# Own semaphores per stage, expert weights in 2 MB loads of 16 KB pieces, and layer 1's memory keys and values made in the first stage

## The chip, the cores and the metric

The kernel runs on one core of a Trainium2 chip. The metric is the device time of one execution in microseconds; a median of several executions is given. The engines of a core named below are TensorE (PE, with PEld for its weight loads), VectorE (DVE), ScalarE (ACT), GpSimd (POOL) and SyncE (SP). Inputs and output are float32.

## The reference

Two blocks run one after the other on 256 tokens of width 1024. The first has two layers. Each layer mixes the tokens (layer 0: a gated projection with a spatial gate over chunks of 128 tokens; layer 1: dilated attention), adds attention over 256 memory rows, normalises, and then runs a mixture of 16 experts, of which every token takes two. The second block (retention, sparse attention, a recurrent mixer, two feed-forward parts, two layers) is not touched by the change.

```
for layer in range(DEPTH):
    mk = (mem @ w_mem_k[layer]).reshape(B, M, MEM_HEADS, HEAD_DIM)
    mv = (mem @ w_mem_v[layer]).reshape(B, M, MEM_HEADS, HEAD_DIM)
    ...
    att = jnp.concatenate([mix, mo], -1) @ w_out
    x = layer_norm(ALPHA * x + att, ln1_g[layer], ln1_b[layer])
    expert, gate = route(h, w_router, b_router)
    ffn = moe_ffn(h, expert, gate, w_gate[layer], w_up[layer], w_down[layer])   # silu(x wg) * (x wu), then wd
    x = layer_norm(ALPHA * x + ffn, ln2_g[layer], ln2_b[layer])
```

Each of the 16 experts of a layer has three matrices of 1024 x 1024, 12 MB; a layer's experts are 201 MB.

## The kernel before

Every engine runs its own program, stage by stage: A (layer 0's mixing), moe0, B (layer 1's mixing), moe1, and two (the second block). The order is written out by hand; each engine's function of a stage has its prefix (`pe_a`, `s_a`, `v_a`, `g_a`, `sp_a` and so on).

Weights go through a ring of 8 slots of 1 MB (8 KB per partition). SP's program orders the loads: `load` (L485) waits until enough slots have been used (`s_used`), then orders a DMA into the slot. In A, B and two a load is a block of 256 columns, so its contiguous pieces are 1 KB. GpSimd relays: `freed` (L517) waits until a product is complete and adds to `s_used`. Products go to four PSUM banks in turn ("pieces"); a semaphore per bank says that it is full, another that it is free.

Stages A to moe1 share one set of semaphores and counters; at each stage's end all engines pad their counters to a multiple of the ring (`end_of_stream`). Stage two has its own set, and a ring of 5 slots.

An expert stage first routes (`pe_moe` from L1100, `v_moe` from L1259) and then loops over 8 pairs of experts, as many passes as the fullest expert needs (one here: CAP is 64 tokens). A turn of the loop: transposes of the gate matrix, the gather of the pair's tokens (X as TensorE's weights, `pair_rows` taking every second column), gate and up products with the two experts side by side in the columns of the array, transposes of h, down products, and the combine into four accumulating banks. Expert weights are loaded by `one` (L1419, the DMA at L1425) as 256 rows of 1024 values, 1 MB: partition p takes rows 2p and 2p + 1, one piece of 8 KB. TensorE adds to `s_half` when 2 MB (both experts) have been used, and GpSimd relays it. SP orders the first 8 loads of a stage ahead of its loop.

In A, ScalarE's last work is a square root for the norm; then `s_moe(0)` orders 20 small parameter loads and two norm loads (L1786, L776) and copies half of x's transposes (L636). Memory keys and values of a layer are made at the start of its own mixing stage by `memory_kv`; the transposed memory `MEMT` stays in the arena until then. In A's spatial gate (L845) each head has two matmuls of 64 columns, one per chunk. The arena is 21760 values per partition; during an expert stage its end is unused.

Of the kernel before, what the change touches and what calls it, by code (L numbers as in the profile page):

```python
# [29 lines left out]
I32 = mybir.dt.int32  # L30
# [4 lines left out]
P = 128  # L35
# [5 lines left out]
HD = 64  # L41
# [26 lines left out]
RAW, HIGHS = 5, 3  # L68
BANKS = 4
# [11 lines left out]
for _k, _v in PV_ROWS.items():  # L81
# [8 lines left out]
        ("pe", "jobs"): 24, ("pe", "pieces"): 12, ("pe", "v2p"): 1,  # L90
        ("v", "jobs"): 24, ("v", "pieces"): 12,
        ("s", "jobs"): 24, ("s", "pieces"): 12,
        ("g", "jobs"): 24, ("g", "pieces"): 12, ("g", "half"): 9,
        ("sp", "jobs"): 24,
    },
    "moe1": {
        ("pe", "jobs"): 24, ("pe", "pieces"): 12, ("pe", "v2p"): 1,
        ("v", "jobs"): 24, ("v", "pieces"): 12,
        ("s", "jobs"): 24, ("s", "pieces"): 12,
        ("g", "jobs"): 24, ("g", "pieces"): 12, ("g", "half"): 9,  # L100
        ("sp", "jobs"): 24,
# [97 lines left out]
def build(nc, a, out, regions=("A", "moe0", "B", "moe1", "two"), layers_two=LAYERS):  # L199
    (c1_at, _), (c2_at, _) = constants()  # L200
    NC = max(max(v[1] for v in c1_at.values()), max(v[1] for v in c2_at.values()))
    with ExitStack() as ctx:
# [57 lines left out]
        def stage_semaphores(tag):  # L260
# [3 lines left out]
                    [sem(f"slot_loaded{s}{tag}") for s in range(SLOTS)],  # L264
# [4 lines left out]
        FIRST, SECOND = stage_semaphores(""), stage_semaphores("_two")  # L269
        s_full, s_free, s_slot, s_acc_full, s_acc_free, s_used, s_v2p, s_a2p, s_v2a, s_a2v = FIRST  # L270
# [11 lines left out]
        s_half = sem("expert_rows_used")  # L282
        s_load = {n: sem(f"loaded_{n}") for n in
# [6 lines left out]
        class Engine:  # L290
# [13 lines left out]
            def second(self):  # L304

                use(SECOND)
                self.jobs, self.pieces = Ring(RAW), Ring(BANKS)
                self.next_high, self.in_high = 0, {}
                for k, v in self.c.items():
                    if not k.startswith("l_"):  # L310
                        v.n, v.base = 0, 0
# [52 lines left out]
            def jobs_pad_check(self):  # L364
                assert self.pieces.n % BANKS == 0 and self.jobs.n % SLOTS == 0, (self.name, self.pieces.n, self.jobs.n)
# [40 lines left out]
        class Tensor(Engine):  # L406
# [8 lines left out]
            def hold(self, b=0):  # L415


                self.mm(ps[:, b, 0:1], ident, ident[:, 0:1], start=True, stop=True)

# [19 lines left out]
            def gemm_tok(self, act, kc=KC, n=BLK, col=0, width=None, slot=None):  # L439
# [9 lines left out]
                for t in range(T):  # L449
                    for k in range(kc):  # L450
                        last = self.mm(ps[:, b, t * BLK:t * BLK + n], act[:, k, t * P:(t + 1) * P],
                                       w[:, k, col:col + n], start=(k == 0), stop=(k == kc - 1))
                last.then_inc(s_full[b], 1)
# [17 lines left out]
        class Stream(Engine):  # L471
            before = None

            def second(self):

                self.before = self.jobs
                super().second()

            def first_slots_free(self):

                n = self.jobs.n
                if self.before is not None and n <= RAW:
                    self.e.wait_ge(FIRST[5], self.before.rounds * SLOTS + self.before.n + n)

            def load(self, src, n, width):  # L485
# [3 lines left out]
                self.first_slots_free()  # L489
                self.e.wait_ge(s_used, self.in_use())  # L490
# [3 lines left out]
            def in_use(self):  # L494
# [3 lines left out]
                return n if isinstance(r, int) and r == 0 else r * SLOTS + n  # L498
# [76 lines left out]
        QM, MK, MV = lay(2, SEQ), lay(2, SEQ), lay(T, MEM_W)  # L575
# [8 lines left out]
        lay = Layout(after_mem)  # L584
        XG, PM, PG, PGT = lay(KC, P), lay(T, P), lay(T, P), lay(SEQ)
# [16 lines left out]
        NPASS = sb("n_passes", [1, 1], I32)  # L602
# [37 lines left out]
        def pe_scores(heads, q, k):  # L640
            for h in heads:
                b = pe.take()
                pe.e.wait_ge(s_free[b], pe.emptied())
                for t in range(T):
                    last = pe.mm(ps[:, b, t * SEQ:(t + 1) * SEQ], q(h)[:, t * P:(t + 1) * P], k(h),
                                 start=True, stop=True)
                last.then_inc(s_full[b], 1)
# [135 lines left out]
        def memory_kv(l):  # L783
# [2144 lines left out]
```

## Time and profile before

| | us |
|---|---|
| median of 3 executions | 3056.08 (3055.98 to 3057.8) |
| the profiled execution | 3066.24 |
| its span, first to last instruction | 3064.4 |
| TensorE busy | 2724.0 (89%) |
| VectorE busy | 1158.8 (38%) |
| ScalarE busy | 786.6 (26%) |

The page divides the span into 40 slices of 76.6 us. The granted clock of TensorE was 0.954 of full speed over the span. By the timeline, stage A ends near 161 us, the first expert loop runs from 196 to 665 us, B ends near 835 us, the second loop runs from 868 to 1338 us, and the second block fills the rest. Idle time of an engine that is not the bound costs nothing; what counts is which wait ends last.

### The profile page before, as it was taken

The page shows a single profiled execution, that of the slowest core. Times are in us where ns is not written, and L with a number is a line of the kernel's source. Part 1 is how long each engine was busy: PE and PEld are TensorE (multiplying, and loading weights), DVE is VectorE, ACT ScalarE, POOL GpSimd, SP SyncE. Part 2 cuts the span into 40 slices and gives each one's busy share as a digit, 9 for nine tenths or more (in the row PEclk, how much of TensorE's full clock was granted, in tenths as well). Part 3 has the DMA queues.
Part 4 walks back from the last instruction along what each step waited for, and adds up shares of the span by engine and source line. Part 5 has one row for each costly group of instructions (what it writes and reads, how often), then busy time and mean ns, then how long its engine had stood idle before and what let it go on. Part 6 is the DMA issues. An engine that isn't in the chain of part 4 may idle for free.

```text
span 3064.4 us, 44961 instructions
## 1 busy us (share of the span) xinstructions
PE 2724.0 (89%) x18948; PEld 2089.2 (68%) x18948; DVE 1158.8 (38%) x1768; ACT 786.6 (26%) x971; POOL 0.2 (0%) x4
## 2 busy tenths in 40 slices
PE   7878888889678888869989899989899898999898
PEld 6643433348434333339989789889799897898897
DVE  0220100123311001035556756445445567564454
ACT  1110101102201011024334442243343343422433
POOL 0000000000000000000000000000000000000000
PEclk9879999999889999989999899999899998998999
DMA  7159999993269999975554332346455543322453
GB/s 246 71 223 420 421 422 422 422 395 110 83 250 419 422 422 422 421 274 193 174 168 141 110 111 71 111 140 204 144 190 169 164 152 110 111 71 84 154 176 124
DMA packets 286112, 684.46 MB, mean 223 GB/s; under 512 B 11898, under 2 KB 217474, under 8 KB 236548
## 3 DMA queue, kind: packets, MB, share of 16 engines
q1 hardware_dynamic: 279776, 669.03, 58.3%
q10 hardware_dynamic: 6180, 13.14, 1.2%
q8 instruction: 123, 2.02, 0.3%
q14 instruction: 33, 0.27, 0.0%
HBM read 681.08 MB, written 1.05 MB: 223 GB/s over the span
## 4 chain that ended last, share of the span: by engine, by line
PE 72%; DMA 15%; DVE 7%; ACT 2%; issue 1%; DVEq 1%; ACTq 1%; SPq 0%; POOLq 0%; PEldq 0%
PE psum L421 70%; DMA weight_ring<-in_w_down 8%; DMA weight_ring<-in_w_up 7%; PE psum L429 2%; DVEq L543 1%; DVE weight_ring_parts L1563 1%; DVE arena_parts L1633 1%; DVE small L666 1%; DVE arena L664 1%; ACT h_tok L1535 0%; SPq L1425 0%; DVE arena L1356 0%; ACT L770 0%; DVE arena L2600 0%; ACTq L865 0%
## 5 line engine op out<-in xcount | busy, mean ns | idle before, releaser
L421 PE MATMUL psum<-weight_ring,arena 128*64 128x512 f32 (+1 forms) x3584 | 798.8, 564 | 126.1 <-DMA weight_ring<-in_w_down 43.3
L421 PEld LDWEIGHTS psum<-weight_ring,arena 128*64 128x64 f32 (+1 forms) x3584 | 346.7, 144 | 552.8 <-issue 537.9
L421 PE MATMUL psum<-x_chan_parts,weight_ring_parts 128*128 128x256 f32 x2944 | 564.9, 282 | 14.9 <-DVE arena_parts L1633 12.2
L1563 DVE TENSOR_TENSOR weight_ring_parts<-weight_ring,weight_ring_parts 128x2048 fp32r<-128x2048 f32 x186 | 425.8, 2290 | 368.1 <-ACT weight_ring_parts L1555 365.9
L421 PE MATMUL psum<-weight_ring_parts,arena_parts 128*128 128x256 f32 (+1 forms) x2272 | 559.2, 326 | 0.0
L1555 ACT ACTIVATE weight_ring_parts<-weight_ring 128x2048 fp32r<-128x2048 f32 x186 | 356.2, 1916 | 599.5 <-POOLq L523 433.8
L421 PEld LDWEIGHTS psum<-x_chan_parts,weight_ring_parts 128*128 128x128 f32 x2944 | 470.1, 190 | 18.3 <-DVE arena_parts L1633 13.6
L421 PEld LDWEIGHTS psum<-weight_ring_parts,arena_parts 128*128 128x128 f32 x2272 | 403.6, 190 | 35.0
L421 PE MATMUL psum<-weight_ring_parts,x_chan_parts 128*128 128x256 f32 x2048 | 381.3, 288 | 7.4 <-DVE arena_parts L1633 4.0
L421 PE MATMUL psum<-arena_parts,weight_ring_parts 128*128 128x256 f32 x1312 | 372.2, 284 | 0.0
L421 PEld LDWEIGHTS psum<-weight_ring_parts,x_chan_parts 128*128 128x128 f32 x2048 | 321.3, 192 | 14.2 <-DVE arena_parts L1633 4.6
L421 PE MATMUL psum<-arena 64*64 64x64 f32 (+7 forms) x3600 | 273.5, 268 | 24.4 <-DVE arena L763 11.7
L421 PEld LDWEIGHTS psum<-arena 64*64 64x64 f32 (+3 forms) x3600 | 195.2, 150 | 91.2 <-issue 32.8
L421 PEld LDWEIGHTS psum<-arena_parts,weight_ring_parts 128*128 128x128 f32 x1312 | 249.2, 190 | 1.3
L1364 DVE TENSOR_TENSOR arena<-arena,psum 128x512 f32<-128x512 f32 x32 | 22.0, 688 | 493.4 <-PE psum L421 492.1
L1244 ACT ACTIVATE arena<-psum 128x512 f32<-128x512 f32 x32 | 19.1, 597 | 427.4 <-PE psum L421 427.4
L429 PE MATMUL psum<-tables,arena 128*128 128x128 f32 x472 | 82.3, 313 | 45.1 <-DVE arena L702 28.4
L429 PEld LDWEIGHTS psum<-tables,arena 128*128 128x128 f32 x472 | 63.5, 174 | 85.7 <-issue 58.1
L1373 DVE COPY arena<-psum 128x512 f32<-128x512 f32 x16 | 11.1, 692 | 283.9 <-PE psum L421 283.9
L1563 DVE TENSOR_TENSOR weight_ring_parts<-weight_ring,h_tok_parts 128x2048 fp32r<-128x2048 f32 x32 | 73.3, 2290 | 73.3 <-ACT h_tok_parts L1555 73.3
L421 PE MATMUL psum<-arena_parts,h_tok_parts 128*128 128x256 f32 x320 | 90.1, 282 | 0.0
L421 PE MATMUL psum<-x_chan_parts,h_tok_parts 128*128 128x256 f32 x320 | 89.7, 280 | 0.0
(275 smaller groups left out, 1935.2 us busy)
## 6 DMA issues: line engine op xcount, KB each, us to landing
weight_ring<-in_w_gate SPq DMA_DIRECT2D x128, 1024.0 KB, 11.0
weight_ring<-in_w_up SPq DMA_DIRECT2D x128, 1024.0 KB, 12.5
weight_ring<-in_w_down SPq DMA_DIRECT2D x128, 1024.0 KB, 14.0
weight_ring<-in_w_in SPq DMA_DIRECT2D x70, 1024.0 KB, 5.2
weight_ring<-in_ffa_w_in SPq DMA_DIRECT2D x44, 1024.0 KB, 7.4
weight_ring<-in_ffb_w_in SPq DMA_DIRECT2D x44, 1024.0 KB, 6.5
weight_ring<-in_ffa_w_out SPq DMA_DIRECT2D x22, 1024.0 KB, 5.0
weight_ring<-in_ffb_w_out SPq DMA_DIRECT2D x22, 1024.0 KB, 4.9
```

What stands on the lines that cost most here:

```text
L421: return nc.tensor.matmul(*args, **kw)
L429: last = nc.tensor.transpose(ps[0:cols, b, lo:lo + rows], src, ident[0:rows, 0:rows])
L543: self.e.drain()
L664: nc.vector.scalar_tensor_tensor(BUF["scores"][:, i], heads2(b), SCALE, more, ALU.mult, ALU.add).then_inc(s_free[b], 1)
L666: nc.vector.tensor_reduce(MX[:, h, :], BUF["scores"][:, i], AX.X, ALU.max)
L1244: nc.scalar.activation(SILU[:, half, :], ps[:, b, :], ACT.Silu).then_inc(s_free[b], 1)
L1364: nc.vector.tensor_tensor(HG[:, half * 512:(half + 1) * 512], SILU[:, half, :], ps[:, b, :], ALU.mult).then_inc(s_free[b], 1)
L1373: nc.vector.tensor_copy(YD[:, 512:1024], ps[:, b, :]).then_inc(s_free[b], 1)
L1555: nc.scalar.activation(HIGH[buf], ring[:, sl, :], ACT.Copy).then_inc(s_hi, 1)
L1563: nc.vector.tensor_tensor(ring_parts[:, sl, :], ring[:, sl, :], f32(HIGH[buf]), ALU.subtract).then_inc(s_split, 1)
L1633: last = nc.vector.scalar_tensor_tensor(dst[:, c + j, :], ps[:, b, j * SEQ:(j + 1) * SEQ], gain[:, c + j:c + j + 1], f32(high[:, c + j, :] ...
```

## The change

1. Semaphores. Each of the five stages has its own set (`SEMS`), with ring sizes 8, 6, 8, 6 and 5. `stage(name)` switches an engine to a set and starts its counters at zero; the padding at the stages' ends and the matmul `hold` before stage two are gone. The first loads of a stage wait (`wait_slot`) on the old stage's count of used slots, for the memory they will overwrite.
2. Expert weights. A load is 512 rows, 2 MB: partition p takes rows 4p to 4p + 3, one piece of 16 KB. There are six slots: two in the unused end of the arena, four made of pairs of ring slots. `every_fourth` takes the place of `pair_rows` for X and h. TensorE reports 4 MB at a time. SP orders six loads ahead of the loop; the two in the arena wait for a new semaphore `s_room`, which TensorE raises with the first `w_out_a` matmul in A and the first memory score in B.
3. Layer 1's memory keys and values are made in A: the keys behind the scores, ahead of the spatial gate, the values behind the four `w_out_a` products; ScalarE copies them into H. B no longer makes them.
4. The spatial gate has one matmul of 128 columns per head.
5. `NPASS` has a second value, which SP reads.

```
-        ("pe", "jobs"): 24, ("pe", "pieces"): 12, ("pe", "v2p"): 1,
+        ("pe", "jobs"): 12, ("pe", "pieces"): 12, ("pe", "v2p"): 1,
...
+        RING_OF = {"A": SLOTS, "moe0": EXPERT_SLOTS, "B": SLOTS, "moe1": EXPERT_SLOTS, "two": RAW}
+        SEMS = {r: stage_semaphores("_" + r, slots) for r, slots in RING_OF.items()}
...
+            def wait_slot(self, held=()):
+                if self.jobs.n > self.jobs.size:
+                    self.e.wait_ge(s_used, self.in_use())
+                elif held:
+                    used, old = self.before
+                    last = max(old.n - 1 - (old.n - 1 - q) % old.size for q in held)
+                    n = old.size + last + 1
+                    r = old.rounds
+                    self.e.wait_ge(used, n if isinstance(r, int) and r == 0 else r * old.size + n)
...
-                self.first_slots_free()
-                self.e.wait_ge(s_used, self.in_use())
+                self.wait_slot(() if self.before is None else (2 + s // 2,))
...
+        EXPERT_ROWS = [view(13568, 4, D), view(17664, 4, D)] + \
+            [ring[:, 2 * i:2 * i + 2, :].rearrange("p s (k n) -> p (s k) n", n=D) for i in range(4)]
...
         def pe_a():
-            pe_scores(MH, mem_q, mem_k)
+            pe_scores(MH, mem_q, mem_k(0))
+            pe.gemm_chan(MEMT)
...
-                    for c in range(T):
-                        last = pe.mm(ps[:, b, j * P + c * HD:j * P + (c + 1) * HD], SWT[:, h, :],
-                                     UG[:, c, SG + h * HD:SG + (h + 1) * HD], start=True, stop=True)
+                    last = pe.mm(ps[:, b, j * P:(j + 1) * P], SWT[:, h, :],
+                                 UG[:, :, SG + h * HD:SG + (h + 1) * HD], start=True, stop=True)
...
-            for _ in range(4):
-                pe.gemm_tok(CAT)
+            for n in range(4):
+                pe.gemm_tok(CAT, first_inc=None if n else s_room)
+            pe.gemm_tok(MEMT)
+            pe.e.wait_ge(s_free[(pe.pieces.n - 1) % BANKS], pe.read_out(pe.pieces.n - 1))
...
         def s_a():
             s_root()
+            copy_piece(s, MK[1])
             s.skip(3)
...
             s_root()
+            copy_piece(s, MV[1])
...
         def sp_a():
             sp.blocks(a["w_in_a"], 0, 2 * SG + MEM_W)
+            sp.blocks(a["w_mem_k"][1], 0, MEM_W)
             sp.blocks(a["w_out_a"], 0, D)
+            sp.blocks(a["w_mem_v"][1], 0, MEM_W)
...
         def pe_b():
-            memory_kv(1)["pe"]()
...
-            pe_scores(MH, mem_q, mem_k)
+            pe_scores(MH, mem_q, mem_k(1), first_inc=s_room)
...
-                for j in range(4):
+                for j in range(2):
                     for m in range(2):
...
-                                                 row_pair(slots[e])[:, kk, half * 512:(half + 1) * 512],
+                                                 EXPERT_ROWS[slots[e]][:, kk, half * 512:(half + 1) * 512],
...
         def sp_moe(l):
-                src = a[w][l, bass.ds(pr * 2 + e, 1), j * 2 * P:(j + 1) * 2 * P, :]
+                src = a[w][l, bass.ds(pr * 2 + e, 1), j * 4 * P:(j + 1) * 4 * P, :]
-                sp.e.wait_ge(s_used, sp.in_use())
+                if sp.jobs.n <= 2:
+                    sp.e.wait_ge(s_room, l + 1)
+                else:
+                    sp.wait_slot((2 * (sl - 2), 2 * (sl - 2) + 1))
+                sp.e.dma_start(EXPERT_ROWS[sl], src.rearrange("o (p k) n -> p (o k) n", p=P)).then_inc(s_slot[sl], 16)
...
+            def first_six(pr):
+                for j, w in ((0, "w_gate"), (0, "w_up"), (1, "w_gate")):
+                    for e in range(2):
+                        one(w, e, j, pr)
+            def other_six(pr):
+                for j, w in ((1, "w_up"), (0, "w_down"), (1, "w_down")):
+                    for e in range(2):
+                        one(w, e, j, pr)
```

## Rows read from the trace of the kernel before

**Rows 1.** The page: TensorE's busy time, and the GB/s of 40 slices.
```profile
PE 2724.0 (89%) x18948; PEld 2089.2 (68%) x18948; DVE 1158.8 (38%) x1768; ACT 786.6 (26%) x971; POOL 0.2 (0%) x4
...
GB/s 246 71 223 420 421 422 422 422 395 110 83 250 419 422 422 422 421 274 193 174 168 141 110 111 71 111 140 204 144 190 169 164 152 110 111 71 84 154 176 124
```
**Rows 2.** The chain that ended last: start us, us, what (two neighbouring pairs).
```profile
330.41 12.54 DMA weight_ring<-in_w_up
...
390.07 12.53 DMA weight_ring<-in_w_up
```
**Rows 3.** DMA queues, 400 to 600 us: packets, MB, share of 16 engines.
```profile
DMA packets 11585, 84.35 MB, mean 422 GB/s; under 512 B 1289, under 2 KB 1289, under 8 KB 1289
...
q1 hardware_dynamic: 11585, 84.35, 101.3%
```
**Rows 4.** Windows: length, busy PE, PEld, DVE, ACT, POOL, PE clock, DMA share, GB/s.
```profile
95.00:100.00 5.00, 0.00 (x0) 0.00 (x0) 3.51 (x12) 2.70 (x8) 0.00 (x0) 0.50 0.00 0
...
190.00:195.00 5.00, 4.46 (x26) 4.26 (x24) 0.51 (x1) 1.88 (x2) 0.00 (x0) 0.68 0.00 0
...
670.00:675.00 5.00, 5.00 (x25) 4.41 (x24) 4.76 (x10) 0.20 (x1) 0.00 (x0) 1.00 1.10 348
```
**Rows 5.** Timeline of one pair, TensorE and SP: start us, us, instruction, idle before.
```profile
408.98 7.36 PE L421 MATMUL psum<-weight_ring,arena 128*64 128x512 f32 x32 [1.06 <-issue]
...
422.65 3.65 PE L421 MATMUL psum<-weight_ring,arena 128*64 128x512 f32 x16 [1.35 <-DMA weight_ring<-in_w_down]
...
429.99 3.93 PE L421 MATMUL psum<-arena,x_tok 128*128 128x128 f32 x32
435.21 16.10 PE L421 MATMUL psum<-weight_ring,arena 128*64 128x512 f32 x74 [1.29 <-DVEq L550]
...
438.94 0.91 SPq L1425 DMA_DIRECT2D weight_ring<-in_w_gate  x2
442.38 0.83 SPq L1425 DMA_DIRECT2D weight_ring<-in_w_up  x2
```
**Rows 6.** Timeline of SP's queue around the start of the first loop.
```profile
152.65 1.16 SPq L1425 DMA_DIRECT2D weight_ring<-in_w_up  x2
199.52 1.66 SPq L1425 DMA_DIRECT2D weight_ring<-in_w_gate  x2
```
**Rows 7.** Timeline of TensorE, stage A to the first loop.
```profile
103.12 10.51 PE L421 MATMUL psum<-arena 128*128 128x64 f32 x48 [11.70 <-DVE arena L763]
...
123.83 27.89 PE L421 MATMUL psum<-weight_ring,arena 128*128 128x256 f32 x128 [0.75 <-ACT arena L636]
160.68 3.67 PE L429 MATMUL psum<-tables,x_tok 128*128 128x128 f32 x16 [8.96 <-DVE x_tok L763]
165.37 6.98 PE L421 MATMUL psum<-router_weights,x_chan 128*128 128x16 f32 x32 [1.02 <-ACT x_chan L636]
...
195.79 17.39 PE L421 MATMUL psum<-weight_ring,arena 128*64 128x512 f32 x80 [1.33 <-DVEq L550]
```
**Rows 8.** Timeline of ScalarE: first of its orders, and its first x copies.
```profile
155.65 0.78 ACTq L1786 DMA_DIRECT2D parameter_rows<-in_rwkv_mu  x2
...
164.06 1.21 ACT L636 ACTIVATE x_chan<-psum 128x256 f32<-128x256 f32 x4 [8.21 <-issue]
```
**Rows 9.** Timeline of TensorE and VectorE, first loop to B.
```profile
661.36 3.65 PE L421 MATMUL psum<-weight_ring,arena 128*64 128x512 f32 x16 [1.33 <-DMA weight_ring<-in_w_down]
...
676.95 2.48 DVE L763 SCALAR_TENSOR_TENSOR x_tok<-x_tok,small,norm_gain_bias 128x1024 f32<-128x1024 f32 x2
...
685.27 48.61 PE L421 MATMUL psum<-x_chan,weight_ring 128*128 128x256 f32 x224 [0.85 <-DVE x_chan L634]
```
**Rows 10.** Timeline of TensorE: first and last expert matmuls of the second loop, stage two.
```profile
868.01 21.09 PE L421 MATMUL psum<-weight_ring,arena 128*64 128x512 f32 x96 [1.30 <-DVEq L550]
...
1333.95 3.65 PE L421 MATMUL psum<-weight_ring,arena 128*64 128x512 f32 x16 [1.47 <-DMA weight_ring<-in_w_down]
...
1352.08 0.59 PE L421 MATMUL psum<-tables 128*128 128x1 f32 x2 [10.62 <-DVE x_tok L763]
```

More of the change, by code:

```diff
@@ L68 @@
 RAW, HIGHS = 5, 3
+EXPERT_SLOTS = 6
 BANKS = 4
@@ L302, in __init__, with stage @@
                     self.c["l_" + k] = Counter(s, 16)
-            def second(self):
-                use(SECOND)
-                self.jobs, self.pieces = Ring(RAW), Ring(BANKS)
+            def stage(self, name):
+                use(SEMS[name])
+                self.jobs, self.pieces = Ring(RING_OF[name]), Ring(BANKS)
                 self.next_high, self.in_high = 0, {}
-                for k, v in self.c.items():
-                    if not k.startswith("l_"):
-                        v.n, v.base = 0, 0
+                for k in ("acc", "accf", "v2p", "a2p", "v2a", "a2v"):
+                    self.c[k].n, self.c[k].base = 0, 0
             def all(self):
@@ L452, in gemm_tok @@
                                        w[:, k, col:col + n], start=(k == 0), stop=(k == kc - 1))
+                        if first_inc and t == 0 and k == 0:
+                            last.then_inc(first_inc, 1)
                 last.then_inc(s_full[b], 1)
@@ L646, in pe_scores @@
                                  start=True, stop=True)
+                    if first_inc and h == heads[0] and t == 0:
+                        last.then_inc(first_inc, 1)
                 last.then_inc(s_full[b], 1)
@@ L1166, in body @@
                             pe.e.wait_ge(s_slot[slots[-1]], pe.landed())
-                        for kk in range(2):
+                        for kk in range(4):
                             for half in range(2):
@@ L1189, in body @@
                     pe.e.wait_ge(s_free[b], pe.emptied())
-                for j in range(4):
+                for j in range(2):
                     slots = []
@@ L1194, in body @@
                         pe.e.wait_ge(s_slot[slots[-1]], pe.landed())
-                    for kk in range(2):
+                    for kk in range(4):
                         for half in range(2):
@@ L1259, in v_moe @@
         def v_moe(l):
+            v.stage(f"moe{l}")
             copy_channels(v, 1, XT, KC)
@@ L1393, in g_moe @@
         def g_moe(l):
+            g.stage(f"moe{l}")
             g.skip(6)
@@ L1399, in body @@
                 g.pad()
-                for _ in range(6):
+                for _ in range(2):
                     g.e.wait_ge(s_half, g.c["half"].next())
@@ L1406, in body @@
                 g.skip(2)
-                for _ in range(3):
+                for _ in range(1):
                     g.e.wait_ge(s_half, g.c["half"].next())
@@ L2717, in pe_two @@
             pe.e.wait_ge(s_v2p, pe.c["v2p"].next())
-            pe.hold()
-            pe.second()
+            pe.stage("two")
             pe_params()
@@ L2746, in s_two @@
             s.e.dma_start(C[:, P:a["tables2"].shape[1]], a["tables2"][:, P:]).then_inc(s_load["tables2"], 16)
-            s.second()
+            s.stage("two")
             s.skip()
@@ L2770, in v_two @@
         def v_two():
-            v.second()
+            v.stage("two")
             v_params()
@@ L2802, in g_two @@
         def g_two():
-            g.second()
+            g.stage("two")
             g.skip()
@@ L2818, in sp_two @@
         def sp_two():
-            sp.second()
+            sp.stage("two")
             for l in range(layers_two):
@@ L2861, in _ @@
         def _(e):
-            for stage in (FIRST, SECOND):
-                use(stage)
+            for stage in RING_OF:
+                use(SEMS[stage])
                 for b in range(BANKS):
@@ L2879, in _ @@
         def _(e):
-            for stage, slots in ((SECOND, RAW), (FIRST, SLOTS)):
-                use(stage)
+            for stage, slots in RING_OF.items():
+                use(SEMS[stage])
                 e.sem_inc(s_used, slots)
```

174 lines of the change are left out of this document (75 added, 99 removed).

## The prediction

> **What bounds the kernel now.** I read the page first: the slices show two plateaus at 422 GB/s, slices 5 to 8 and 13 to 16, while TensorE is busy 89% of the span [rows 1]. The plateaus are the two expert stages. In the chain of waits TensorE there stands behind the landing of expert weights once for up and once for down in every pair of experts, and the same wait comes back after 390.07 - 330.41 = 59.66 us [rows 2]. A pair is 24 pieces of 1 MB, 25.17 MB, and 25.17 MB in 59.66 us are 421.9 GB/s, the rate of a 200 us window in the middle, where the transfer engines are busy 101% of the time [rows 3]. So in the loops the bound is the rate of the DMA engines, and a faster TensorE would bring nothing. Elsewhere (stages A and B, routing, and the whole second block after 1340 us) TensorE and its hand-offs to VectorE and ScalarE are the bound. The reader is to see next that the DMA engines do nothing just before a loop starts: share 0.00 in 190 to 195 us [rows 4], since all eight slots were ordered by 153.8 us and the next order waits until 199.52 us, when the first slot has been used [rows 6].
>
> **The loops, before.** From the first expert matmul to the end of the last down matmul the first loop takes 661.36 + 3.65 - 195.79 = 469.2 us [rows 7, 9], the second 1333.95 + 3.65 - 868.01 = 469.6 us [rows 10]. The sum behind it: 3.73 us until the first two slots are ordered again (199.52 - 195.79), 92 loads of 2 MB (96 less the four that are there at the start) at 59.66/12 = 4.97 us, 457.4 us, and 3.65 us for the last matmuls, 464.8 us; the 4.4 us that are left are the way from an order to its first data and from the last data to TensorE. I split them 2.2 and 2.2.
>
> **16 KB pieces.** A piece of 1 KB goes at 348 GB/s when the engines are full (670 to 675 us [rows 4]), which is 16 x 1024 B / 348 = 47.1 ns on each of 16 engines. A piece of 8 KB at 422 GB/s [rows 3] takes 310.6 ns. A line through both has 9.4 ns fixed and 36.8 ns per KB (36.76 ps per byte). At 16384 B it gives 611.7 ns, 428.5 GB/s; 4 MB take 9.79 us instead of 9.94. The line is carried beyond its last point, so the ends of this price are 9.94 us (nothing gained) and 9.6 us (as much below the line as it lies below no gain); I take the line, since both points lie in long stretches of full queues.
>
> The Trainium skill, "DMA: Bandwidth & Descriptors", section "Why small descriptors are slow", puts the cost of a packet at 3 cycles beside one per 32 B. That is 3 in 259 for 8 KB and 3 in 515 for 16 KB, a gain of 0.6% where the line gives 1.5%; by it the two loops would give back some 5 us rather than 14 for this part. For 1 KB it would be 3 in 35, 8.6%, where the rows show 348 against 422, so the measured cost of a piece is larger than the page has it.
>
> **Six slots of 2 MB.** 12 MB instead of 8 can be there when a loop starts. In stage A the two arena slots open with the first w_out_a matmul (now 123.83 us [rows 7]), slot 2 is open by then, slots 3 and 4 open with the second and fourth w_out_a product, slot 5 with the product for memory V. That last order comes near 151 us, its 2 MB need 4.9 us, and the loop starts near 192 us: 30 us of cover. In B the last three open with the last w_out_b product, 40 us ahead of 868.01 us. What remains to be loaded per loop is 45 groups of 4 MB. The price: TensorE frees 4 MB at a time. 16 matmuls take 3.44 us in a row (the orders at 438.94 and 442.38), and the first order stands 0.3 us behind its 16 (438.94 against 435.21 + 3.44 [rows 5]). So the first order comes after 6.9 + 0.3 us, and the last group keeps TensorE 6.9 to 7.4 us (32 in 7.36 [rows 5]; I take 7.1) instead of 3.65. Sum: 7.2 + 45 x 9.79 + 4.4 + 7.1 = 459.3 us, 9.9 us less than now, in the second loop the same: 19.8 us. Without any gain of rate it would be 466.2 us, 3.0 us less per loop.
>
> **Does the stream stay full?** Three groups are queued, 29.4 us. From the last data of a pair the next slot is ordered and answered after 2.2 + 7.1 + the turn + 7.1 + 0.3 + 2.2. The turn (combine, transposes, gather, copies) is 435.21 - 426.30 = 8.9 us [rows 5]. Sum 27.8 us, 1.6 us to spare. The same sum for the kernel before is 2.2 + 3.65 + 8.9 + 3.45 + 0.3 + 2.2 = 20.7 us against 19.9 queued, and [rows 3] show no gap; so the sum is some 0.8 us too dark, and the cover is about 2 us. TensorE alone needs 12 x 3.44 + 8.9 = 50 us for a pair, and some 3 us for h, against 58.7 for the data.
>
> **Stage A.** Memory K of layer 1 goes into the hole of TensorE before 103.12 us [rows 7]: the scores end 11.70 us earlier, at 91.4, and the product takes 6.9 us (seven of its kind in 48.61 us [rows 9]). Its bank comes free with the first exponentials, which I put 2 us behind the scores, an estimate; so it ends near 100.5. Its cover is 2.6 us; without that cover it would cost what it overruns. Its load stands ahead of w_out_a on SP's queue, but these are needed at 123.83 us, and the DMA engines are idle at 95 us [rows 4]. Two things follow. The clock of TensorE, which fell to 0.50 while it idled (95 to 100 us [rows 4]), should stay at its upper level, and the spatial gate now has 24 instructions of 128 columns instead of 48 of 64, which took 10.51 us. The gather in a pair runs 32 such in 3.93 us, 0.123 us each at the upper clock [rows 5]: 2.9 us, 7.6 us less; at half clock twice that, 5.9 us, 4.6 less. What follows up to 123.83 us ran partly at half clock and gets some tenths back between waits for VectorE. I take 8.0 us, ends 4.6 and 12.
>
> Memory V goes behind w_out_a, into the hole before 160.68 us. It ends 1.8 us before the norm does. But its copy is the next thing on ScalarE's queue, and behind it are queued the 20 parameter rows and two norm loads that ScalarE issues, and behind these its half of the x copies, for which TensorE waits ahead of the router. Now the row of issues runs from 155.65 to 164.06 us, 8.4 us, and the copies start at 164.06 [rows 8]; the router at 165.37 [rows 7]. After: w_out_a ends at 143.7, memory V at 150.8, its copy at 151.6, the issues at 160.0, the copies at 161.2, the router at 161.4. So of the 8.0 us 4.0 are left: a wait of TensorE on ScalarE takes the place. Ends for A as a whole: 0.5 (half clock) and 8.
>
> **Stage B and the rest.** The two memory products, 14.1 us, go, but they ran beside VectorE's norm, which ends at 676.95 + 2.48 = 679.43 us [rows 9]; only 3.1 us stood out of it. TensorE now idles there, so the clock falls as it does in A: the 16 transposes take 3.7 us as at 160.68 [rows 7], twice what they would at the upper clock, and the first projections run at half clock for 1 to 2 us. 679.5 + 3.7 + 0.9 = 684.1, plus that loss, against 685.27: I take 0.5 us gained, ends -1 and 3.1. B's first 4 MB are ordered when the last group but one is used, 14 us and a norm ahead of their use: nothing; nor for the second block, whose weights are wanted some 20 us behind the loop. The matmul that held the stage boundary, 0.59 us [rows 10], ran beside ScalarE's issues and is costed at nothing, 0.6 us if they did not cover it. Two one-element copies on VectorE: 0.2 us lost.
>
> Sum: -19.8 - 4.0 - 0.5 + 0.2 = -24.1 us. The profiled execution took 3066.24 us around a span of 3064.4, 0.3% over the median of 3056.08; its terms scale by as little. Forecast 3056.1 - 24.1 = 3032 us.
>
> **Rivals.** (1) The rate does not rise: what limits at 422 GB/s is not the piece. For it: the share is already 101%. Against it: 348 GB/s at the same full queues with 1 KB pieces. -24.1 + 2 x 6.9 = -10.3, 3046 us. By the Trainium skill's rule above the time would lie between, near 3041 us. (2) Slower: the turn outgrows its cover. The gather and the transposes of h now read every fourth column instead of every second, as weights of TensorE. If that doubled the gather (3.93 to 7.86 us), 14 turns would each lose 1.9 us or more, 27 us, the two first gathers, partly at half clock, 4 to 8 us each, say 12, and -24 turns into +15: 3071 us. It decides from about 3 us more per gather. Against it: with every second column the gather costs 0.123 us per instruction, what 128 columns of plain data cost at that clock. (3) The early loads don't come: if a slot opens late and only 8 MB are there, 9.9 us are lost per loop and the gain is 4 us, 3052 us. For it: six waits in one queue; against it: 30 us of cover.
>
> **How the numbers follow.** Forecast 0.66, its own range 3025 to 3040 (A and B's ends, the half of the rate). Rival 1 with the rule beside it 0.14, rival 2 0.07, rival 3 and its like 0.07, better than 3024 0.06. The range leaves out the last three: 3024 to 3047. 0.2%, 6 us, is what a measurement of this kernel can tell from no change: faster 0.86, same 0.07, slower 0.07.
>
> **What would show it.** In windows inside a loop: 427 to 429 GB/s, or 422 (rival 1), or slices with less and a DMA share under 1 (rival 2). A pair period of 58.7 us in the chain. First expert matmul near 192 us. In 95 to 120 us granted clock 1.00, gate matmuls 24 in about 3 us. A wait of TensorE on ScalarE's copies ahead of the router of about 7 us. B's first projection 19 us behind the last down matmul. The forecast is wrong if the loops are not 459 us, above all.

## The result and the profile after

The changed kernel takes 3074.27 us (median of 6 runs, 3069.74 to 3081.76) and the kernel before 3056.23 us in the same comparison: ratio 1.006, 95% interval 1.0044 to 1.0075. I had forecast 3032 us. The time lies where rival 2 ended: the turn outgrows its cover.

The profiled execution took 3069.74 us, its span 3067.9. Set beside the rows of before it divides like this (the third column is the first experiment):

| us | before | changed | copied X |
|---|---|---|---|
| first expert product at | 195.79 | 191.99 | 189.86 |
| loop 1, first expert to end of last down product | 469.2 | 478.5 | 456.8 |
| B, from there to layer 1's first expert product | 203.0 | 202.4 | 200.9 |
| loop 2 | 469.6 | 480.0 | 457.1 |
| from there to the end | 1726.8 | 1715.1 | 1721.1 |

The last line is work that no kernel here touches. It came out between 1713 and 1729 us in 13 of the 14 kernels here (1740.7 in experiment 2), so what an edit is worth is read from the other lines. There the change gained 3.8 us in A and 0.6 in B and lost 9.3 and 10.4 us in the loops: 15.3 us lost in all, where the medians say 18.0.

The page of the changed kernel, the GB/s of its slices, which answer to [rows 1]: the plateaus are no longer level.

```profile
GB/s 273 164 193 413 407 404 418 408 369 55 150 236 413 401 415 414 407 313 151 193 155 160 124 110 71 84 161 170 185 151 197 155 157 124 110 70 84 153 177 124
```

Windows of the changed kernel (length, busy PE, PEld, DVE, ACT, POOL, PE clock, DMA share, GB/s), three in a row of the first loop and one of the second:

```profile
256.00:260.00 4.00, 4.00 (x20) 1.41 (x18) 0.00 (x0) 0.00 (x0) 0.00 (x0) 1.00 0.82 348
260.00:264.00 4.00, 4.00 (x22) 1.48 (x20) 0.00 (x0) 0.00 (x0) 0.00 (x0) 1.00 0.61 172
264.00:268.00 4.00, 4.00 (x22) 1.49 (x20) 0.00 (x0) 0.00 (x0) 0.00 (x0) 1.00 1.01 434
...
900.00:925.00 25.00, 21.10 (x92) 8.57 (x89) 4.53 (x14) 2.48 (x3) 0.00 (x0) 1.00 1.01 431
```

Where the DMA engines are full they move 431 GB/s, more than the 422 of [rows 3] and than the 428.5 I expected. But once a pair they run out of orders (share 0.61 in 260 to 264 us), while TensorE is busy all the time. SP orders nothing between these two:

```profile
239.50 0.87 SPq L1446 DMA_DIRECT2D weight_ring<-in_w_gate  x2
260.76 0.91 SPq L1446 DMA_DIRECT2D arena<-in_w_up  x2
```

The chain that ended last, with the pair's period (398.06 - 335.62 = 62.44 us against 59.66 in [rows 2]; over six pairs it is 61.4):

```profile
335.62 18.12 DMA weight_ring<-in_w_down
...
366.51 7.48 PE psum L418 x32
...
398.06 18.27 DMA weight_ring<-in_w_down
```

The chain now holds one wait for data per pair, not two, and the gather with 7.48 us. TensorE's timeline of a turn, beside [rows 5], the gather's weight loads of 200 to 640 us (count, busy us, mean ns), and a window at the start of the gate products:

```profile
232.33 7.09 PE L418 MATMUL psum<-weight_ring,arena 128*64 128x512 f32 x32 [2.69 <-DMA weight_ring<-in_w_down]
239.35 3.70 PE L418 MATMUL psum<-arena 128*128 128x512 f32 x8
...
243.11 7.63 PE L418 MATMUL psum<-arena,x_tok 128*128 128x128 f32 x32
252.04 8.64 PE L418 MATMUL psum<-arena 128*64 128x512 f32 x32 [1.30 <-DVEq L555]
```
```profile
L418 PEld LDWEIGHTS psum<-arena,x_tok 128*128 128x128 f32 x224 | 52.8, 329 | 0.0
```
```profile
252.00:255.00 3.00, 2.96 (x8) 1.14 (x10) 0.00 (x0) 0.00 (x0) 0.00 (x0) 0.50 1.00 426
```

The gather takes 7.63 us instead of 3.93, the turn (end of the last down product to the next gate product) 252.04 - 239.42 = 12.6 us instead of 8.9. And the 32 gate products behind it take 8.64 us, not 7.09, since the granted clock is at 0.50 when they begin (the window). That is so in 8 of the 16 pairs (8.45 to 8.79 us). The transposes of h, which rival 2 named too, cost nothing more: eight take 1.52 us at the step of four and 1.51 at the step of two, with 0.56 us for four of their weight loads in both.

Stage A, TensorE and ScalarE, beside [rows 7, 8]:

```profile
101.63 4.54 PE L418 MATMUL psum<-arena 128*128 128x128 f32 x24 [2.36 <-DVE arena L772]
...
151.42 2.35 PE L426 MATMUL psum<-tables,x_tok 128*128 128x128 f32 x16 [2.09 <-issue]
159.74 6.98 PE L418 MATMUL psum<-router_weights,x_chan 128*128 128x16 f32 x32 [5.98 <-ACT x_chan L643]
...
149.37 0.83 ACTq L1805 DMA_DIRECT2D parameter_rows<-in_rwkv_mu  x2
...
158.43 1.21 ACT L643 ACTIVATE x_chan<-psum 128x256 f32<-128x256 f32 x4 [8.47 <-issue]
```

### The profile page after: what moved, and what is told of

It is laid out like the page before. It is cut to its first block, busy times and chain, and to the rows that moved or that the text cites. A ratio compares the mean times of both kernels' runs of the same rounds, so it can differ in the third digit from the quotient of the medians.

```text
span 3067.9 us, 43977 instructions
## 1 busy us (share of the span) xinstructions
PE 2774.9 (90%) x18922; PEld 2134.8 (70%) x18922; DVE 1157.8 (38%) x1770; ACT 787.1 (26%) x971; POOL 0.2 (0%) x4
## 4 chain that ended last, share of the span: by engine, by line
PE 78%; DMA 10%; DVE 6%; ACT 2%; issue 1%; DVEq 1%; ACTq 1%; SPq 0%; PEldq 0%; POOLq 0%
PE psum L418 76%; DMA weight_ring<-in_w_down 10%; PE psum L426 2%; DVEq L548 1%; DVE weight_ring_parts L1582 1%; DVE arena_parts L1652 1%; DVE small L675 1%; ACT h_tok L1554 0%; DVE arena L673 0%; DVE arena L1373 0%; ACT L779 0%; DVE arena L2619 0%; ACTq L881 0%; ACT weight_ring_parts L1574 0%; DVE small L758 0%
## 5 line engine op out<-in xcount | busy, mean ns | idle before, releaser
L418 PE MATMUL psum<-weight_ring,arena 128*64 128x512 f32 (+1 forms) x2560 | 581.7, 567 | 57.0 <-DMA weight_ring<-in_w_down 45.5
L418 PE MATMUL psum<-x_chan_parts,weight_ring_parts 128*128 128x256 f32 x2944 | 565.7, 282 | 15.2 <-DVE arena_parts L1652 12.6
L418 PE MATMUL psum<-arena 64*64 64x64 f32 (+6 forms) x4568 | 491.6, 340 | 36.9 <-DVEq L555 20.9
L418 PEld LDWEIGHTS psum<-weight_ring,arena 128*64 128x64 f32 (+1 forms) x2560 | 269.6, 151 | 351.9 <-issue 325.1
L418 PEld LDWEIGHTS psum<-arena 64*64 64x64 f32 (+3 forms) x4568 | 264.9, 143 | 239.2 <-issue 189.7
L418 PE MATMUL psum<-arena,x_tok 128*128 128x128 f32 x512 | 121.9, 400 | 0.0
L418 PEld LDWEIGHTS psum<-arena,x_tok 128*128 128x128 f32 x512 | 120.7, 329 | 0.0
```

The source lines that it names most:

```text
L418: return nc.tensor.matmul(*args, **kw)
```

## The experiments

**1. Plain columns for the gather.** VectorE copies X once per expert stage while TensorE routes.

```diff
+        XP = lay(T, KC, P)
...
             v.stage(f"moe{l}")
             copy_channels(v, 1, XT, KC)
+            for t in range(T):
+                nc.vector.tensor_copy(XP[:, t].rearrange("p (j k) q -> p j k q", k=4),
+                                      X[:, t, :].rearrange("p (j q k) -> p j k q", q=P, k=4))
...
-    last = pe.mm(ps[:, b, kk * P:(kk + 1) * P], every_fourth(X[:, t, :], k), PM[:, t, :],
+    last = pe.mm(ps[:, b, kk * P:(kk + 1) * P], XP[:, t, k, :], PM[:, t, :],
```

> The changed kernel with one edit: while TensorE runs the router, VectorE copies X once per expert stage into a spare place with the columns of each group next to each other, and the gather reads its weights from there as plain 128 columns. Loads, slots, order and everything else stay. Theory (the gather's stride outgrows the queue's cover): the gather falls from 7.63 to 3.9 us, the turn from 12.6 to 8.9 us, the queue no longer runs empty, and the loops go at the full rate that single windows of the changed kernel already show (431 GB/s, 9.73 us per 4 MB): 7.2 + 45 x 9.73 + 4.4 + 7.1 = 456.6 us each instead of 478.5 and 480.0, pair period 58.4 us, in all 3026 to 3035 us. Rival (the stream has holes for another reason, such as 4 MB being freed at a time or the clock's drops inside the loop): the gather gets short, but the windows stay near 411 GB/s, and the time stays over 3060 us.

Measured: 3027.46 us against 3059.01 before, 0.9884 (0.9859 to 0.9909; here and below the ratio is an estimate of its own, not the quotient of the two medians). Its timeline, chain and a window:

```profile
288.56 8.78 PE L418 MATMUL psum<-weight_ring,arena 128*64 128x512 f32 x32 [2.70 <-DMA weight_ring<-in_w_down]
...
301.03 3.74 PE L418 MATMUL psum<-arena 128*128 128x128 f32 x32
306.09 7.09 PE L418 MATMUL psum<-arena 128*64 128x512 f32 x32 [1.33 <-DVEq L555]
```
```profile
327.50 19.43 DMA weight_ring<-in_w_down
...
385.93 19.51 DMA weight_ring<-in_w_down
```
```profile
400.00:600.00 200.00, 178.22 (x829) 79.01 (x827) 18.86 (x57) 21.95 (x29) 0.00 (x0) 0.97 1.01 430
```

The gather takes 3.74 us, the gate products behind it 7.09 in all 16 pairs, the period is 58.43 us, the engines are full over 200 us, and the loops take 456.8 and 457.1 us where I had expected 456.6. The rival falls: 4 MB freed at a time does not starve the queue.

**2. The old kernel with the new columns.** Only `pair_rows(X[:, t, :], k)` becomes the changed kernel's view of X.

> The kernel before with one edit: the gather takes every fourth column of X as its weights instead of every second. The loads stay as they are, so the gathered columns don't belong to the weight rows that they meet: the expert outputs are other numbers than the reference's, the work is the same. Theory (the cost hangs on the step between columns, and the old queue has no cover to spare either): the gather goes from 3.93 to 7.6 us and the pair period from 59.66 to between 61.4 and 63.3 us; over 14 turns 25 to 50 us, the first two gathers with 3 to 8 us each on top, in all 3085 to 3115 us. Rival (the longer gather comes from something else in the change, the arena slots that DMAs write beside X or the larger loads): the gather stays at 3.9 us and the time at 3056 us.

Measured: 3107.94 us, 1.0144 (1.0119 to 1.0169).

```profile
375.43 7.63 PE L421 MATMUL psum<-arena,x_tok 128*128 128x128 f32 x32
```
```profile
450.00:475.00 25.00, 23.38 (x109) 8.95 (x107) 0.00 (x0) 1.19 (x2) 0.00 (x0) 1.00 0.91 376
```

The same 7.63 us without any other part of the change. The loops take 491.0 and 494.1 us, 21.8 and 24.5 more, 3.1 to 3.5 us per turn for 3.7 us of gather. That is not all length: in 7 of the 16 pairs the products behind the gather begin at a dropped clock (22.3 to 22.5 us for 96 instead of 20.8, for instance), which happens in no pair of the kernel before. In the first loop, behind its first pair, a pair without such a drop takes 62.2 to 62.3 us and one with it 63.9 to 64.1, against 59.66, so with the clock up the old queue covered some 1.1 us of the 3.7. The cost hangs on the columns alone.

**3. Length without the step.** Experiment 1 with the gather executed twice (`for t in [*range(T), *range(T)]`). The expectation says that the gathered tokens are doubled; they are not, since the second round begins its sums anew.

> The kernel of the copied X with the gather's matmuls executed twice, 64 instead of 32 (the second round adds the same products once more, so the gathered tokens are doubled: other numbers than the reference's, more work on purpose). It separates the length of the turn from the stride. Theory (length alone counts): 7.9 us of gather, a turn of 12.8 us, and the loops of the changed kernel come back: about 479 us each, in all 3068 to 3078 us. Rival (strided reads disturb the transfers or the products in another way too): the gather is as long, but the loops keep at least half of what the copy gave, under 3055 us.

Measured: 3063.66 us, 1.0009 (0.9989 to 1.0029).

```profile
247.29 7.31 PE L418 MATMUL psum<-arena 128*128 128x128 f32 x64
255.93 7.09 PE L418 MATMUL psum<-arena 128*64 128x512 f32 x32 [1.32 <-DVEq L555]
```

The loops take 470.3 and 470.2 us: 13.5 and 13.1 us more than in experiment 1 for 7 x 3.57 = 25.0 us of gather, so the queue covers some 1.65 us a turn. But the changed kernel's loops take 8 to 10 us more than these. Length is some six tenths of the loss (13.5 of 21.7 us, 13.1 of 22.9), and neither theory nor rival, as I had put them, has the rest. In the changed kernel the gather is 0.32 us longer still (2.2 us a loop), and five of seven turns of loop 1 have gate products at a dropped clock, 7.7 us together. Here no gate group is above 7.09. In loop 2 only two turns have it (3.2 us) and the first gate group of the loop (1.7 us); there the clock fell in the last down group instead, in six of seven turns (8.52 to 8.79 us) against four here. So none of the 14 turns of the changed kernel is without a drop just ahead of the gather or behind it; here five are.

**4. How long a turn may be.** Experiment 1 with every second column group of the gather executed twice, 48 matmuls.

> The kernel of the copied X with every second column group of the gather executed twice, 48 matmuls instead of 32 (the repetition begins its sum anew). Doubling the whole gather lengthened the turn by 3.57 us and each loop by 13.4 us, 1.9 us per turn. Theory (a threshold: the queue covers the first 1.6 to 2 us and every further one is lost): the gather takes 5.5 us, the pair period stays at 58.5 us or up to 0.2 us above it, the loops take 457 to 459 us, and in all 3031 to 3036 us, of which 4 us come from the two first gathers, which nothing covers. Rival (no threshold, each us of turn costs about half a us): loops near 463.5 us, in all over 3043 us.

Measured: 3040.13 us, 0.9933 (0.991 to 0.9956), loops of 464.6 and 461.9 us. The loops are the rival's (463.5), the total lies between the two (3036 and 3043), so the threshold as I had put it did not come out. TensorE's timeline shows pairs of both kinds:

```profile
251.62 7.09 PE L418 MATMUL psum<-arena 128*64 128x512 f32 x32 [1.30 <-DVEq L555]
...
293.51 8.78 PE L418 MATMUL psum<-weight_ring,arena 128*64 128x512 f32 x32 [2.71 <-DMA weight_ring<-in_w_down]
...
312.80 7.09 PE L418 MATMUL psum<-arena 128*64 128x512 f32 x32 [1.29 <-DVEq L555]
...
353.39 7.09 PE L418 MATMUL psum<-weight_ring,arena 128*64 128x512 f32 x32 [2.70 <-DMA weight_ring<-in_w_down]
...
371.02 7.09 PE L418 MATMUL psum<-arena 128*64 128x512 f32 x32 [1.33 <-DVEq L555]
```

The first of these pairs takes 61.18 us, the second 58.22, and the next one, with a last down group of 8.78 us again, 60.21. The down group in front of the turn waits 2.7 us for its 4 MB and then runs at 7.09 or, with the clock dropped, at 8.78 us. Those 1.7 us lie on the same way as the turn and eat into the cover. Of the six pairs between the first and the last of this loop the three with such a group take 61.18, 60.21 and 58.89 us, the three without 58.22, 58.29 and 58.53: with the clock up the 1.8 us of gather that this run adds are covered whole. Experiment 3 has the same split: the five pairs without such a group take 58.8 to 59.1 us, the nine with it 60.5 to 62.0. So by an estimate from these periods, against 58.43, the cover is near 3 us with the clock up and on average 1 us or less behind a dropped group. This is a reading of two traces, an argument and no proof: nothing was run that holds the clock.

**5, 6. The size of the pieces.** Experiment 1 (5) and the changed kernel itself (6) with two pieces of 8 KB per partition in each 2 MB load:

```diff
-    sp.e.dma_start(EXPERT_ROWS[sl], src.rearrange("o (p k) n -> p (o k) n", p=P))
+    sp.e.dma_start(EXPERT_ROWS[sl].rearrange("p (h k) n -> p h k n", k=2),
+                   src.rearrange("o (h p k) n -> p (o h) k n", p=P, k=2))
```

> The kernel of the copied X with 2 MB loads that consist of two pieces of 8 KB per partition instead of one of 16 KB (rows 2p, 2p + 1 of each half; X and h are split to match). Slots, orders and semaphores stay, only the piece is halved. Theory (a fixed cost per piece, as the rows of 1 KB and 8 KB pieces show): full windows at 422 GB/s instead of 431, 9.94 us per 4 MB instead of 9.73, so 45 x 0.21 = 9.5 us more per loop, 19 us more in all than the kernel of the copied X, some 3048 us. Rival (the 431 GB/s come from fewer and larger loads, not from the piece): windows stay at 431 GB/s and the time within 4 us of the kernel of the copied X.

> The changed kernel, without the copy of X, but with every 2 MB load made of two pieces of 8 KB per partition (rows 2p, 2p + 1 of each half). X and h are then read at every second column again, as in the kernel before; semaphores, slots, order of loads stay as changed. It asks what the change is worth without its 16 KB pieces, and whether a step of two columns is free. Theory (step two costs nothing worth naming, step four doubles the gather and drops the clock behind it): gather 3.9 us against 3.74 with plain columns, gate products behind it at 7.09 us in every turn, full windows at 425 GB/s, in all 3038 to 3046 us, some 30 us below the changed kernel. Rival (the loads' layout itself, not the step of the columns, costs the turns their cover): pair periods stay over 60.5 us and the time over 3060 us.

Measured: 3039.30 us, 0.9918 (0.9893 to 0.9943), and 3040.81 us, 0.9936 (0.9915 to 0.9956). The window of 5, and of 6 with its gather:

```profile
250.00:450.00 200.00, 176.09 (x820) 75.75 (x818) 15.69 (x45) 19.00 (x26) 0.00 (x0) 0.98 1.01 425
```
```profile
250.00:450.00 200.00, 176.95 (x822) 76.89 (x820) 15.70 (x45) 19.00 (x26) 0.00 (x0) 0.98 1.01 425
```
```profile
302.50 3.93 PE L418 MATMUL psum<-arena,x_tok 128*128 128x128 f32 x32
```

8 KB pieces in 2 MB loads go at 425 GB/s, in the 1 MB loads of before at 422, 16 KB pieces at 430. So neither theory (422 GB/s, 3048 us) nor rival (431) of experiment 5 came out: the pieces are worth 425 to 430, and the larger load is the likely reason for 422 to 425, though the kernel before differs from experiment 5 in more than that. 4 MB take 9.87 instead of 9.75 us, 45 times 0.115 is 5.2 us a loop; measured are 6.9 and 5.9 (1.4 of the first is the last down group at a dropped clock). In 6 the loops take 464.0 and 463.7 us, as in 5: a step of two columns costs 3.93 against 3.74 us and no more. The change without its 16 KB pieces is faster than before by 0.6%.

**7, 8. How the step sets the weight load.** The changed kernel with a step of three and of eight columns, one execution each.

> The changed kernel with the gather's weights at a step of three float32 columns (12 bytes) instead of four (16 bytes); other columns are gathered than the reference wants, the amount of work is the same. Weight loads of 128 columns take 189 ns with plain columns, 196 at a step of two, 328 to 329 at a step of four. Theory (lines of 16 bytes: a load is slowed by how often it comes to a new line; three of four accesses here open one, half of them at a step of two): 230 to 300 ns a load, a gather of 5 to 6.8 us. Rival (the time grows with the distance, or with any step that is no power of two): 328 ns or more. Rival (a plain limit at 16 bytes and above): 196 ns, 3.9 us.

> The changed kernel with the gather's weights at a step of eight float32 columns (32 bytes); other columns are gathered than the reference wants, the amount of work is the same. Theory (lines of 16 bytes: at a step of four every access already opens a new line, so a wider step costs no more): 329 ns a weight load, 7.6 us of gather, the time of the changed kernel. Rival (the time grows with the distance): 450 ns or more, a gather over 11 us, and a total over 3110 us.

Measured: 3039.5 and 3073.36 us (before: 3059.86). The gather's weight loads in 200 to 640 us, first at a step of two (before), then three, then eight:

```profile
L421 PEld LDWEIGHTS psum<-arena,x_tok 128*128 128x128 f32 x224 | 26.9, 196 | 0.0
```
```profile
L418 PEld LDWEIGHTS psum<-arena,x_tok 128*128 128x128 f32 x224 | 39.6, 261 | 0.0
```
```profile
L418 PEld LDWEIGHTS psum<-arena,x_tok 128*128 128x128 f32 x224 | 54.1, 336 | 0.0
```

189 ns plain (the combine's loads; 191 for these and the copied gather's together in experiment 1), then 196, 261, 329 and 336 ns at steps of 2, 3, 4 and 8; the gather takes 3.74, 3.93, 5.74, 7.63 and 7.81 us at steps of 1, 2, 3, 4 and 8. The gate products behind it begin at a dropped clock in 6 of 16 pairs at a step of eight and in none at a step of three. From two to four each column more costs some 66 ns a load; from one to two and beyond four next to nothing. Lines of 16 bytes fit, a growth with distance does not, nor a limit that begins at 16 bytes.

The Trainium skill, "SBUF — State Buffer", section "Door 1: The DMA port swizzle", gives the memory lines of 16 bytes, of which an access pattern should hit each at least twice. The trace agrees: with two float32 of a line used the load is nearly as good as plain (196 ns against 189), with one it is not (329). The same passage puts the stride that is free at 4 float32, and there the measurement differs: at four the load costs 329 ns against 189, and at three 261.

**9, 10, 11. Stage A and the moved products**, all on experiment 1: 9 orders the 20 parameter rows (`s_load_rows()`) behind the router's exponentials, 10 makes layer 1's memory keys and values at B's start again, 11 does both.

> The kernel of the copied X, and ScalarE orders the 20 parameter rows behind the router's exponentials instead of ahead of its half of the x copies. In the kernel of the copied X the orders stand from 149.11 to 157.4 us, the x copies begin at 158.29 and the router waits 6.00 us for them. Theory (the orders are what TensorE waits for, as I said for stage A): the copies begin near 152 us, the router near 153.7 instead of 159.60, and all that follows comes 5 to 6 us earlier: 3019 to 3023 us. Rival (the wait comes back later: the router's clock is at half there, or the orders now hold up ScalarE's work in the routing): the first expert product comes less than 2 us earlier, 3025 to 3029 us.

> The kernel of the copied X with one part of the change undone: layer 1's memory keys and values are made at the start of stage B again, beside VectorE's norm, and their weights are loaded there. Theory (my ledger of the move: some of stage A's gain, the clock ahead of the gate, hangs on the keys' product; B loses the 0 to 3 us that stand out of the norm): first expert product 1.5 to 3 us later than 189.86 us, gate products 24 in over 5 us, B from the end of the last down product to the first expert product of layer 1 at 201 to 204 us against 200.89; in all 3029 to 3033 us. Rival (the values' product and its copy only put ScalarE's orders further back, so undoing the move makes the router earlier): the first expert product comes up to 3 us earlier and the time is 3022 to 3027 us.

> The kernel of the copied X with both edits on stage A: ScalarE orders the 20 parameter rows behind the router's exponentials, and layer 1's memory keys and values are made in stage B again. Apart, the first put the first expert product at 184.97 us, the second at 187.61 us (from 189.86), and the second made B 1.1 us longer. Theory (the move out of B gains nothing in A, it only puts the orders ahead of the x copies further back; once they are gone the router follows the norm and its transposes in both): the first expert product within 1.5 us of 184.97 us, B at 202 us instead of 200.9, in all 3025 to 3028 us. Rival (the keys' product keeps the clock up and so is worth 2 to 5 us of stage A when the orders don't hide it): first expert product at 187 to 190 us, over 3028 us.

Measured: 3025.37 us, 0.9883 (0.9859 to 0.9906); 3031.34 us, 0.9903 (0.9881 to 0.9925); 3026.25 us, 0.9886 (0.9864 to 0.9908). The time of 9 is the rival's (3025 to 3029), those of 10 and 11 the theories'. But edits of 1 to 5 us don't show in such intervals, so the traces have to say it; 9, then 10:

```profile
154.69 7.01 PE L418 MATMUL psum<-router_weights,x_chan 128*128 128x16 f32 x32 [0.85 <-DVE x_chan L642]
...
184.97 7.09 PE L418 MATMUL psum<-arena 128*64 128x512 f32 x32 [1.32 <-DVEq L555]
```
```profile
157.48 6.98 PE L418 MATMUL psum<-router_weights,x_chan 128*128 128x16 f32 x32 [2.27 <-ACT x_chan L644]
...
187.61 7.09 PE L418 MATMUL psum<-arena 128*64 128x512 f32 x32 [1.32 <-DVEq L555]
```

In 9 the router waits for nothing of ScalarE's and the first expert product comes at 184.97 us instead of 189.86, 4.9 us earlier, near the 5 to 6 of the theory. In 10 it comes 2.25 us earlier, the rival's side: undoing the move helps A, because the values' copy no longer stands ahead of the orders; B gets 1.0 us longer (201.9), and loop 1 takes 458.7 us, its last down group at a dropped clock (8.78 us). In 11 it comes at 185.95, and B takes 201.4 us, 0.2 more than in 9. So with the orders out of the way the move is worth 1.2 us, and with them in the way it costs 1.3; both are small beside what the clock does in A, where the 24 gate products take 2.94 us in 9 and 4.47 in 11. Experiment 9 is the best in the traces' ledger; by the times it is not told apart from 1 or 11.

**12. The gate at 64 columns**, on experiment 1, as in the kernel before.

> The kernel of the copied X with the spatial gate as two matmuls of 64 columns per head and not one of 128 (part 4 of the change undone). There 24 instructions take 4.47 us. Theory (an instruction of 64 columns costs the same as one of 128, as 48 in 10.51 us at half clock and 24 in 4.47 us suggest): 48 take 8 to 10 us, stage A ends 4 to 5 us later, and since the router waits for ScalarE's orders behind the values' copy, which move along with A, the first expert product comes as much later: 3031 to 3033 us. Rival (64 columns take half the time of 128): 4.5 to 5.5 us, nothing lost, 3027 us.

Measured: 3032.52 us, 0.9906 (0.9879 to 0.9932).

```profile
101.56 10.50 PE L418 MATMUL psum<-arena 128*128 128x64 f32 x48 [2.36 <-DVE arena L773]
```
```profile
101.50:106.00 4.50, 4.44 (x21) 4.45 (x22) 2.92 (x12) 0.00 (x0) 0.00 (x0) 0.51 0.00 0
```

The first expert product comes at 197.23 us, 7.4 us later; the profiled spans differ by 7.1 us, the medians by 5.1. The theory had 4 to 5. The 48 instructions of 64 columns take 0.219 us each at a clock of 0.50; the 24 of 128 take 2.94 us where the clock is up (five of the eleven kernels that have them), 4.47 where it is at half for the first 3.2 us. The row of 48 stays at half clock to its end (0.50 in 109 to 112 us too), where the row of 24 is through by then; the transposes behind it take 1.91 us in place of 1.04. So the fourth part of the change is worth more here than the moved products.

## Why the prediction was wrong, by its steps

**The step that failed: "Does the stream stay full?"** It took the turn after from the turn before, 8.9 us, although in the diff the gather's weights go from every second to every fourth column. The row I had [rows 5] showed a step of two at the price of plain columns, and I wrote that down as evidence against rival 2. It is evidence about a step of two. The change's step had no row, so its price should have had two ends in the sum; it had one, in a rival with a chance of 0.07. Measured are 7.63 us (I had set 7.86 for the rival) and a turn of 12.6 us, which makes the way from a pair's last data to the next slot's 31.5 us where 29.4 are queued: the stream does not stay full. The loops came out at 478.5 and 480.0 us, not at 459.3. Nor was the step of two quite plain: 0.123 us an instruction against 0.117 in experiment 1.

**The cover** came out as a mean: 1.6 to 2 us by the sum, 1.65 a turn in experiment 3. What I did not have is that this is a mean of turns with near 3 us and turns with little, since a drop of the clock ahead of the turn goes at its cost.

**The rival's sum** came near the measured time, 3071 against 3074, with the wrong parts. It had 27 us for 14 turns and 12 for the two first gathers, which nothing covers. Against the copied X the loops lost 21.7 and 22.9 us, 3.2 a turn and not 1.9, the difference being in the main the drops of the clock ahead of and behind the gather, and the first gathers with what goes before them 2.1 in A and 1.4 in B.

**The rate** was right in direction and a little small: forecast 428.5 GB/s and 459.3 us a loop, measured 430 to 431, and with the gather short 456.8 and 457.1. The line through pieces of 1 and 8 KB carried to 16 KB gave 611.7 ns, measured 16 x 16384 B / 430 GB/s = 609.6. That the larger load probably has a part in it (422 to 425) was not in the sum. Rival 1 (422 stays) falls. By the estimate from the Trainium skill, "DMA: Bandwidth & Descriptors", section "Why small descriptors are slow", the piece should have brought 0.6%; experiments 1 and 5 show 1.2%.

**Six slots**: the orders for the first loop stood at 115 to 150 us and for the second at 800 to 831, so 12 MB were there each time; rival 3 falls. The first re-order came 7.2 us into the loop, as forecast (199.15 - 191.99).

**Stage A**: first expert product forecast near 192, measured 191.99, but 1.5 us of that had been gained by 31 us, before the change, where the first products met a higher clock (7.07 against 8.19 us). The wait for ScalarE was as forecast (router at 159.74, forecast 161.4; 5.98 us of waiting), and experiment 9 shows it as the cause. The gate took 4.54 us, not the 2.9 at the upper clock; I had the half clock, 5.9, as the other end. The keys' product did not keep the clock at 1.00 as I had said: 95 to 120 us show 0.93.

**Stage B**: forecast 0.5 us gained, measured 0.65; its first projection 19.0 us behind the last down product, as written.

## What to carry to other kernels

When a change alters how a matmul's stationary operand is read, the step between its columns is a term of the sum: price it in bytes, for every reader of that data, the ones that the change was not made for above all. If the new step has no row in the trace, give its price two ends and let the worse one into the range; here a copy of X, 2.0 us on an idle VectorE, turned 0.6% slower into 1.2% faster. A stream that is "full" by 2 us is full only as long as no clock falls on the way from a used slot to the next order.

## What the runs showed of the hardware

A weight load of 128 float32 columns costs 189, 196, 261, 329 and 336 ns at steps of 4, 8, 12, 16 and 32 bytes; the 32 matmuls of the gather come to 0.117, 0.123, 0.179, 0.238 and 0.244 us each. A row of such slow loads is often followed by a dropped clock (0.50 to 0.71 in the first 1.5 us of the products behind it), in 8 of 16 pairs of the changed kernel, 7 of 16 in experiment 2 and 6 of 16 at a step of eight, and in none behind twice as many fast loads of about the same length (7.31 against 7.63 us) or at a step of three. Where TensorE waits 2.7 us at a stretch for 4 MB instead of 1.3 us twice for 2 MB [rows 5], the products behind the wait often run at a dropped clock (0.50 to 0.80 in their first 1.5 us), in 12 of 16 pairs of the changed kernel and 6 of 16 with the copy; the mean clock of 200 to 640 us is 0.97 after, with the copy as well, and 1.00 before. Large DMA pieces gain up to the last step seen: 422, 425 and 430 GB/s for 8 KB in 1 MB, 8 KB in 2 MB and 16 KB in 2 MB loads.
